# Retention's sample states: read in the mixer, updated in the two FFNs behind it; 72-row spreads and four-strip reads

## The reference, cut to what matters

```
Retention: S_t = gamma_h S_{t-1} + k_t v_t^T, o_t = q_t S_t
q,k (B,L,H,Dk), v (B,L,H,Dv), s0 (B,H,Dk,Dv)        H = 4, Dk = 256, Dv = 512
mLSTM:     C_t = f' C_{t-1} + i' v k^T                H = 4, Dk = 128, Dv = 256
layer 0:   x += 0.5*SwiGLU_1; x += mixer_ab; x += CrossAttn; x += 0.5*SwiGLU_2
layer 1:   x += 0.5*SwiGLU_1; x += mixer_c;  x += CrossAttn; x += 0.5*SwiGLU_2
```

## Time and profile before

| | |
|---|---|
| median of 3 runs | 1909.96 us (1896.08 to 1912.29) |
| the profiled execution | 1907.95 us; span 1906.1 us |
| PE matmul busy | 1786.1 us (94%) |
| DVE, ACT, POOL busy | 1259.7 (66%), 848.1 (44%), 210.9 (11%) |
| mean granted TensorE clock | 0.978 |
| DMA | 361.01 MB, mean 189 GB/s |
| the chain that ended last | PE 69%, DVE 12%, ACT 11%, issue 4%, DMA 3% |

### The profile page before, as it was taken

One profiled execution on the slowest core, in us unless ns is written; L12 is line 12 of the kernel. 1 busy time (PEld: TensorE's weight loads), 2 busy tenths in 40 slices (PEclk: granted clock), 3 DMA queues, 4 the chain that ended last, 5 costly groups with the idle time before them and its releaser, 6 DMA issues.

```text
span 1906.1 us, 34200 instructions
## 1 busy us (share of the span) xinstructions
PE 1786.1 (94%) x13440; PEld 1629.2 (85%) x13440; DVE 1259.7 (66%) x2241; ACT 848.1 (44%) x1156; POOL 210.9 (11%) x305
## 2 busy tenths in 40 slices
PE   7999988998988899999899999999998889899998
PEld 7999988997765555888699999999976788799998
DVE  5765678785886766558567655765555768667653
ACT  5333455364666644332344334433443642344333
POOL 1001101100110111112020001000311031120001
PEclk9999989999999999999999999999999999999999
DMA  8656735444895698657656656665744467756653
GB/s 226 177 167 177 213 109 158 134 133 124 236 288 171 209 294 286 209 199 274 232 149 181 176 162 195 184 186 154 218 137 134 145 240 247 263 151 185 186 154 115
DMA packets 463585, 361.01 MB, mean 189 GB/s; under 512 B 14633, under 2 KB 435781, under 8 KB 463429
## 3 DMA queue, kind: packets, MB, share of 16 engines
q1 hardware_dynamic: 409904, 254.87, 45.7%
q0 software_dynamic: 20288, 71.94, 11.0%
q10 hardware_dynamic: 33280, 32.65, 5.1%
HBM read 320.95 MB, written 38.66 MB: 189 GB/s over the span
## 4 chain that ended last, share of the span: by engine, by line
PE 69%; DVE 12%; ACT 11%; issue 4%; DMA 3%; ACTq 0%; SPq 0%; POOL 0%; DVEq 0%; POOLq 0%
PE psum L263 19%; PE psum L264 18%; PE psum L265 18%; ACT whi L211 4%; DVE wlo L217 4%; DMA raw<-in_w_xkv 2%; PE psum L1723 2%; ACT hb L1503 1%; PE psum L826 1%; PE psum L480 1%; PE psum L2201 1%; PE psum L591 1%; PE psum L2296 1%; PE psum L1350 1%; DVE sb L1745 1%
## 5 line engine op out<-in xcount | busy, mean ns | idle before, releaser
L217 DVE TENSOR_TENSOR wlo<-raw,whi 128x2048 fp32r<-128x2048 f32 (+2 forms) x261 | 553.4, 2120 | 287.9 <-ACT whi L211 287.1
L263 PE MATMUL psum<-xnh,whi 128*128 128x264 f32 x2328 | 676.0, 290 | 6.7 <-DVE ht L1169 4.3
L264 PE MATMUL psum<-xnl,whi 128*128 128x264 f32 x2328 | 665.5, 286 | 0.0
L265 PE MATMUL psum<-xnh,wlo 128*128 128x264 f32 x2328 | 664.5, 285 | 0.0
L211 ACT ACTIVATE whi<-raw 128x2048 fp32r<-128x2048 f32 (+2 forms) x261 | 460.9, 1767 | 134.3 <-DMA raw<-in_w_xkv 61.0
L263 PEld LDWEIGHTS psum<-xnh,whi 128*128 128x128 f32 x2328 | 444.5, 191 | 25.7 <-issue 24.5
L264 PEld LDWEIGHTS psum<-xnl,whi 128*128 128x128 f32 x2328 | 444.9, 191 | 0.3
L265 PEld LDWEIGHTS psum<-xnh,wlo 128*128 128x128 f32 x2328 | 442.4, 190 | 0.0
L263 PE MATMUL psum<-Hh,whi 128*128 128x264 f32 x704 | 200.9, 285 | 0.0
L265 PE MATMUL psum<-Hh,wlo 128*128 128x264 f32 x704 | 200.0, 284 | 0.0
L264 PE MATMUL psum<-Hl,whi 128*128 128x264 f32 x704 | 199.1, 283 | 0.0
(11 more groups left out here) (559 smaller groups left out, 2930.7 us busy)
## 6 DMA issues: line engine op xcount, KB each, us to landing
raw<-in_w_ffn_in SPq DMA_DIRECT2D x176, 512.0 KB, 4.9
raw<-in_w_in_ab SPq DMA_DIRECT2D x88, 512.0 KB, 4.7
raw<-in_w_ffn_out SPq DMA_DIRECT2D x64, 384.0 KB, 4.0
raw<-in_w_ffn_out SPq DMA_DIRECT2D x64, 320.0 KB, 3.4
sb<-in_state_ret POOLq DMA_DIRECT2D x32, 512.0 KB, 5.8
out<-sb ACTq DMA_DIRECT2D x32, 512.0 KB, 3.4
raw<-in_w_out_ab SPq DMA_DIRECT2D x32, 512.0 KB, 5.1
kc<-in_cache_mem_k POOLq DMA_DIRECT2D x32, 512.0 KB, 6.8
```

Source lines behind the costliest of these rows:

```text
L217: nc.vector.tensor_tensor(wlo[:, c % SLOTS, 0:m], raw[:, c % SLOTS, 0:m], whi[:, c % SLOTS, 0:m].bitcast(F32), ALU.subtract).then_inc(lo_d ...
L263: e.matmul(out, a, hi[:, kk, 0:S.cols], start=first, stop=False)
L264: e.matmul(out, a, lo[:, kk, 0:S.cols], start=False, stop=False)
L265: m = e.matmul(out, b, hi[:, kk, 0:S.cols], start=False, stop=final)
```

## The change

- In the mixer a `RetItem` only loads a state and reads it; the next load waits for the read (`s_used`), not for a store. The spread, the decay, the update and the store are gone from there, and so are the rows of v.
- A read is made of four matmuls of 256 columns: two halves of the key dimension (d) times two halves of the value dimension, each into its own 8 rows at 0, 32, 64 and 96 of bank 5 (`lane`). `RetOut` adds the two d-rows with a matmul against a 0/1 matrix (`group_sum`) in place of the transposes, 16 of them over 104 rows. A head now waits for the copy of the head before it. DVE clears bank 5 once.
- `RetKeep` keeps the samples' k and v. `late_work` places, in FFN 2 of layer 0, the rows of v (`LateRows`, 4 groups) and eight loads (`RetLater`) behind chunk 0, and one `RetUpdate` (spread, load of the state six items ahead, decay, update, store) behind chunks 1, 3, .. 21 and behind chunks 1, 4, 7, 10, 13 of its output projection; the other 16 in the same way in FFN 1 of layer 1.
- Rows and spreads use 72 rows (low part at 64) in place of 40, everywhere.
- mLSTM reads alternate between two groups of rows, which are added by matmuls (`pair_sum`) in place of transposes; `RowsOut` is one copy of 104 rows in place of two of 8. Its first loads wait for the late stores.
- `TURNS` becomes (0, 3, 2, 1).

```diff
-            TURNS = (0, 2, 1, 3)
+            TURNS = (0, 3, 2, 1)
...
+        group_sum = cols[0:104, 16:32].rearrange("p (q b) -> p q b", q=2)
+        sel = place("sel", [72, NS], F32R)
...
-        def spread40(e, out, b, rows):
-
-
-            return e.matmul(out, sel[0:40, b:b + 1].to_broadcast([40, P]), rows, start=True, stop=True)
+                    d = S.dst[64:72, j * 512:(j + 1) * 512]
+                    e.tensor_tensor(d, psum[64:72, S.bank0 + j % 2, :], d.bitcast(F32), ALU.subtract).then_inc(rows_lo, 1)
+
+        def spread72(e, out, b, rows):
+
+
+            return e.matmul(out, sel[0:72, b:b + 1].to_broadcast([72, P]), rows, start=True, stop=True)
...
-            row_of = lambda h: slice(64 + 32 * (h % 2), 64 + 32 * (h % 2) + NS)
+            lane = lambda d, half: slice(32 * (2 * d + half), 32 * (2 * d + half) + NS)
+            part_of = lambda h: slice((h % 2) * 256, (h % 2) * 256 + 256)
...
+                    e.memset(psum[:, 5, :], 0.0).then_inc(qk_made, 1)
...
                 def pool(S, e):
                     j = S.i + SB
                     if j < N_RET:
-                        e.wait_ge(s_out[buf(j)], 16 * (j // SB))
+                        e.wait_ge(s_used, S.i + 1)
                         load_s(e, j)
 
                 def pe(S, e):
                     i = S.i
                     b, h = item(i)
-                    v_row(e, i)
                     if i == 0:
                         e.wait_ge(qk_made, 2)
                     if b == 0:
                         e.wait_ge(q_set, h + 1)
-                        if h >= 2:
-                            e.wait_ge(rr_copied, h - 1)
+                        if h >= 1:
+                            e.wait_ge(rr_copied, h)
                     e.wait_ge(s_in[buf(i)], 16 * (i // SB + 1))
                     for d in range(2):
-                        m = e.matmul(psum[row_of(h), 5, :], qm[:, h % 2, d, b * NS:(b + 1) * NS], sb[:, buf(i), d, :],
-                                     start=b == 0 and d == 0, stop=b == NS - 1 and d == 1)
+                        for half in range(2):
+                            m = e.matmul(psum[lane(d, half), 5, part_of(h)], qm[:, h % 2, d, b * NS:(b + 1) * NS], sb[:, buf(i), d, half * 256:half * 256 + 256],
+                                         start=b == 0, stop=b == NS - 1)
                     m.then_inc(s_used, 1)
+
+            keep_v = place("keep_v", [P, 64 + 128], at=norm_at + 2 * T * 4)
+            keep_k = place("keep_k", [P, 8, NS], at=norm_at + 2 * T * 4 + 768)
+            later = place("later", [P, LB, 2, 512], at=REG + 57344)
+            late_in, late_out = s_in[0:4] + hb_in, s_out[0:4] + hb_out
+            late_base = ret_moves[0:4] + [64] * 4
+            late_out_base = [0] * 4 + [64] * 4
+            v_late = place("v_late", [72, 2048], F32R, at=REG + 49152)
+
+            class RetKeep(Stage):
+
+
+                def dve(S, e):
+                    e.memset(keep_v[:, 0:64], 0.0)
+                    e.tensor_copy(keep_v[:, 64:192].rearrange("p (t b) -> p t b", b=NS), vf[:, :, NP:T])
+                    link(e, "dve", e.tensor_copy(keep_k[:, :, :], ks[:, :, :]))
+
+            class LateRows(Rows72):
+
+
+                def __init__(S, ready):
+                    S.dst, S.n, S.bank0, S.ready = v_late, 4, 6, ready
+                    S.r0 = tot["rows"]
+                    tot["rows"] += S.n
+
+                def pe(S, e):
+                    S.ready(e)
+                    for j in range(S.n):
+                        if j >= 2:
+                            e.wait_ge(rows_lo, S.r0 + j - 1)
+                        for q in range(4):
+                            t = 4 * j + q
+                            e.transpose(psum[0:72, S.bank0 + j % 2, q * P:(q + 1) * P], keep_v[:, 8 * t:8 * t + 72], ident[:, :])
+                            m = e.transpose(psum[0:NS, S.bank0 + j % 2, q * P:(q + 1) * P], keep_v[:, 64 + 8 * t:72 + 8 * t], ident[:, :])
+                        m.then_inc(rows_turned, 1)
+
+            def load_late(e, i):
+                e.dma_start(later[:, i % LB, :, :], sv(A["state_ret"], i)).then_inc(late_in[i % LB], 16)
+
+            class RetLater(Stage):
+
+
+                def __init__(S, free, rows):
+                    S.free, S.rows = free, rows
+
+                def pool(S, e):
+                    S.free(e)
+                    for i in range(LB):
+                        load_late(e, i)
+
+                def pe(S, e):
+                    e.wait_ge(rows_lo, S.rows.r0 + S.rows.n)
+
+            class RetUpdate(Stage):
+
+
+                def __init__(S, i):
+                    S.i = i
+
+                def pool(S, e):
+                    i = S.i - 2
+                    if 0 <= i < N_RET - LB:
+                        e.wait_ge(late_out[i % LB], late_out_base[i % LB] + 16 * (i // LB + 1))
+                        load_late(e, i + LB)
+
+                def pe(S, e):
+                    i = S.i
+                    b, h = item(i)
+                    if i >= 2:
+                        e.wait_ge(s_new, i - 1)
+                    spread72(e, psum[:, 6 + i % 2, :], b, v_late[:, h * 512:(h + 1) * 512]).then_inc(vb_done, 1)
 
                 def keep(S, e, i):
                     e.wait_ge(s_new, i + 1)
-                    e.dma_start(sv(O[9], i), sb[:, buf(i), :, :]).then_inc(s_out[buf(i)], 16)
+                    e.dma_start(sv(O[9], i), later[:, i % LB, :, :]).then_inc(late_out[i % LB], 16)
 
                 def act(S, e):
                     i = S.i
-                    if i >= 2:
-                        S.keep(e, i - 2)
-                    e.wait_ge(s_used, i + 1)
-                    v = sb[:, buf(i), :, :]
+                    if i >= 1:
+                        S.keep(e, i - 1)
+                    e.wait_ge(late_in[i % LB], late_base[i % LB] + 16 * (i // LB + 1))
+                    v = later[:, i % LB, :, :]
                     nc.scalar.activation(v, v, ACT.Copy, scale=gam[item(i)[1]]).then_inc(sdec, 1)
-
-                def update(S, e, i):
+                    if i == N_RET - 1:
+                        S.keep(e, i)
+
+                def dve(S, e):
+                    i = S.i
                     b, h = item(i)
                     e.wait_ge(sdec, i + 1)
                     e.wait_ge(vb_done, i + 1)
                     for d in range(2):
-                        v = sb[:, buf(i), d, :]
-                        ins = e.scalar_tensor_tensor(out=v, in0=psum[:, 6 + i % 2, :], scalar=ks[:, 2 * h + d, b:b + 1], in1=v,
+                        v = later[:, i % LB, d, :]
+                        ins = e.scalar_tensor_tensor(out=v, in0=psum[:, 6 + i % 2, :], scalar=keep_k[:, 2 * h + d, b:b + 1], in1=v,
                                                      op0=ALU.mult, op1=ALU.add)
                     ins.then_inc(s_new, 1)
 
-                def dve(S, e):
-                    if S.i >= 1:
-                        S.update(e, S.i - 1)
-
-
-            class RetLast(Stage):
-
-
-                def dve(S, e):
-                    RetItem(N_RET - 1).update(e, N_RET - 1)
+            def late_work(free):
+
+                rows = LateRows(free)
+                items = [RetUpdate(i) for i in range(N_RET)]
+                first = [rows, RetLater(free, rows)]
+                half = N_RET // 2
+                spots = list(range(1, 22, 2)), list(range(1, 16, 3))
+                at = [{}, {}, {}, {}]
+                for n, it in enumerate(items):
+                    f, m = n // half, n % half
+                    j, c = (0, spots[0][m]) if m < len(spots[0]) else (1, spots[1][m - len(spots[0])])
+                    at[2 * f + j].setdefault(c, []).append(it)
+                at[0].setdefault(0, []).extend(first)
+                return at
+            deferred.append(late_work)
...
-                    e.tensor_scalar(rrow[row_of(h), h // 2, :], psum[row_of(h), 5, :], gam[h], None, ALU.mult).then_inc(rr_copied, 1)
+                    e.tensor_scalar(rrow[0:104, h, 0:256], psum[0:104, 5, part_of(h)], gam[h], None, ALU.mult).then_inc(rr_copied, 1)
...
-                    e.wait_ge(s_new, N_RET - 1)
                     for t in range(16):
-                        r = row_of(t // 4)
-                        m = e.transpose(psum[:, 4 + 2 * (t // 4 % 2), t * NS:(t + 1) * NS], rrow[r, t // 8, (t % 4) * P:(t % 4 + 1) * P], ident[r, r])
+                        m = e.matmul(psum[:, 4 + 2 * (t // 4 % 2), t * NS:(t + 1) * NS], rrow[0:104, t // 4, (t % 2) * P:(t % 2 + 1) * P], group_sum[:, t // 2 % 2, :],
+                                     start=True, stop=True)
...
-            ret_at[0] = [v_rows[1], SSDSample(15)]
+            ret_at[0] = [SSDSample(15)]
             ret_at[1] = [SSDEnd(15), SSDOut()]
-            ret_at[2] = [RetStart()]
+            ret_at[2] = [RetKeep(), RetStart()]
...
```

(19 more changed lines are left out.)

84 lines of the change are left out of this document (39 added, 45 removed).

## The result

The kernel after takes 1873.36 us (median of 4 runs, 1872.77 to 1873.97), the kernel before 1907.51 beside it (1896.08 to 1912.29): a ratio of 0.9841, 95% interval 0.9813 to 0.9869. It is faster, by 34 us of 1907 or 1.6%, clear of the scatter; the forecast was 17.5 us less than before, 1890, in a range of 1866 to 1918 that holds the result. A later set gave 0.9843 (0.982 to 0.9865). The profiled execution has a span of 1871.5 us (before: 1906.1).

What follows compares the result with a forecast made beforehand. The prediction took PE, 69% of the chain that ended last, as the bound, with ACT and DVE setting most gate-projection chunks. Mixer 47, FFNs -34, mLSTM 2.5 and TURNS 2 made 17.5 us saved: 1907.95 to 1890 us, range 1866 to 1918.

Steps and rivals of the forecast that it cites:

- part 2: The FFNs, which take over the spreads and updates: 34 us slower, from spreads 20.5, LateRows 11.5 and DMA 2.
- part 1: The mixer, with shorter state reads and without spreads and updates: 47 us saved.
- Output projection: In the mixer: 19 items save 1.7 us each, plus 4.8 us idle, 37 us before new waits and RetOut.
- Gate projection: In the mixer: ACT's chain sets five chunks, so only 15 us of PE's 22 come through; ends 12 to 24.
- LateRows: Behind chunk 0 of FFN 2: PE stands 10 us for low parts, 1.5 more for a slower clock; 11.5 us lost.
- DMA: In the FFNs: 16.8 MB more loads bring the DMA share to 0.87; 2 us lost, ends 0 and 15.
- TURNS: Head order in the v projection: 8.3 us around against 8.6; 2 us saved over 8 chunks, ends -2 and +5.
- A: The forecast itself, chance 0.5: all terms as summed, 1880 to 1902 us.
- B: Whole kernel, chance 0.2: PE's time comes through everywhere, the gate projection giving its 22 us; 1870 us.
- D: Mixer reads, chance 0.03: four strips don't overlap for accumulating reads, 1.3 us x 32 less saved; 1925 us.
- C: FFNs' output projections, chance 0.17: doubled state traffic makes weights late, 30 to 35 us; slower, 1923 us.
- the wash (E): Whole kernel, chance 0.1: stalls at LateRows and at the heads at their bad ends cancel the gain; 1905 us.

Runs made afterwards that it cites:

- e1: The kernel after with all row spreads over 40 rows as before, nothing else changed; 1886.58 us, ratio 0.9901 to the kernel before.
- e9: The kernel after run again unchanged, as the measure for two other runs; 1870.63 us, ratio 0.9843 to the kernel before.
- e6: The kernel after with a finished head's copy directly behind its last read, not half a chunk later; 1869.46 us, ratio 0.9819 to before.
- e11: The kernel after with 40-row spreads, one-strip reads in both mixers and the old head order, so mainly the move; 1909.68 us, ratio 1.0035 to before.
- e3: The kernel after with retention's reads, RetOut's transposes and the wait for head copies as before; 1888.51 us, ratio 0.991 to before.
- e5: The kernel after with the LateRows groups in three places, behind chunks 0, 2 and 4 of FFN 2; 1868.15 us, ratio 0.982 to before.
- e7: The kernel after with late stores, and late loads behind the first eight, cut to 1 of 128 partitions; 1870.44 us, ratio 0.9829 to before.
- e2: The kernel before with 72-row spreads everywhere and nothing else of the change; 1896.98 us, ratio 0.9962 to the kernel before.
- e4: The kernel after with the head order of before, (0, 2, 1, 3); 1874.25 us, ratio 0.9835 to the kernel before.
- e10: The kernel after with the mLSTM's reads in one group of 8 rows per head and transposes, as before; 1878.17 us, ratio 0.9876 to before.

## Why the prediction was right, and where it was not

The side and the mechanism were right: PE's items leave a stretch that PE sets, and come back smaller in one that PE sets too. The sum was half of what came. Of the 17 us that it lacked, 10 are in the FFNs, from one step, and 7 in cross-attention, for which it had no term; the output projection gave 3 more than forecast and the gate projection 4 less, which about cancels by luck. That the range holds the result owes to its width of 52 us.

**The step that failed** is the first of part 2, "32 spreads of 72 rows cost what those of 40 do (the columns are the same 512): 0.43 + 0.10 + 0.11 = 0.64 us each". The three numbers were right for 40 rows, and e1 shows them again in the FFNs. But of the 0.43 only 0.24 are the columns; the rest, the gap ahead and the delay behind are the price of 40 rows between weights of 128, and 72 rows do not pay it. That is 0.4 us x 32 = 13 us; 11.9 measured, or 8.9 against e9. With 40 rows (e1) the two FFNs took 35.6 us, for the 34 of the forecast; with 72 they took 23.7 in after and 26.7 in e9. The rule was cited in part 1 for the reads, where it changed nothing, and not asked of the very edit that the diff makes for every spread. From it came a second miss, "0" for cross-attention: its 8 pairs of spreads cost 0.39 us less each, 3.1 us in layer 0. After gained 7.4 there. Set beside e1 the stretch seems to refute this, for with 40 rows it is shorter still; but its length goes with the granted clock. The windows are of before, after, e1 and e6:

```profile
784.93:966.69 181.76, 167.84 (x1274) 150.57 (x1273) 109.63 (x245) 62.58 (x83) 29.10 (x49) 0.95 0.62 214
735.48:909.87 174.39, 161.49 (x1274) 147.72 (x1273) 109.42 (x245) 62.62 (x83) 29.07 (x49) 0.98 0.65 223
738.57:909.25 170.68, 160.80 (x1274) 144.21 (x1273) 109.22 (x245) 62.59 (x83) 29.05 (x49) 1.00 0.66 228
730.86:908.96 178.10, 165.48 (x1274) 151.26 (x1273) 109.42 (x246) 62.60 (x83) 29.06 (x49) 0.95 0.63 219
```

At the same 0.95 it takes 181.8 us (before) and 180.6 (e11) with 40 rows and 178.1 (e6) with 72, which agrees with the 3.1. The other 4 of after's 7.4 us go with its clock, 0.98 for 0.95. What raised it is open: PE's wait for one load (`mtok`) alone lasts 1.3 to 4.1 us in these traces, and whether waits lower the clock or a lower clock makes the waits was not told apart.

**Output projection** (forecast 29.5 with the waits and RetOut, measured 32.6). The read came out at 0.55 us as forecast, RetOut takes 3.6 for the 3.9 assumed. The waits: 2.2 us at head 2, as forecast, none at head 3. e3 and e11 split it: the spreads and the waits for updates (the idle 4.8) give 15, the strips 18.

**Gate projection** (forecast 15, measured 11.4). Right in kind: ACT and DVE set the chunks, and e3 and e6 show that 16 us of PE's reads more or less change the stretch by 0.7 us. Wrong in the step "in a chunk that ACT and DVE set anyway, so nothing" for head 1's wait: it lasted 4.07 us, the 4 us forecast, and the chunk behind it gave nothing in place of 2.1; in e6, without the wait, that chunk gives 2.5. (The chunk ahead of it gave 0.3 in after and in e6, so its missing 1.8 have another cause, which is open.) Without the wait the gate projection gives 13.6 us. I read it so: PE's statistics feed ACT's root, so a late PE delays the next turn of the chain, and the clock was lower as well; the two were not told apart.

**LateRows** (11.5, measured 11.6 on PE). Every part came as forecast: the stand behind the second group for ACT's and DVE's evictions (4.91 us), the slower transposes behind it, and the wait for the last low part. The eviction times show 10.9 us by the third chunk behind it (13.9 in e9). e5 takes 4.7 to 5.5 of it back.

**DMA** 2 us: e7 gives 0.7 and 1.9, or 3.4 and 2.2 against e9. **POOL**: its late refills delayed nothing that PE had to wait for. **TURNS** (2 us) and **the rows of v** (3): the evictions show 0.6 up to 456.7 and 4.9 from there to 573.6, of which 1.6 come at 476.8, where e2 too has 1.7, from the spreads of B and C. The whole times of e4 cannot tell TURNS from nothing; by the evictions the 0.6 are its worth. **mLSTM** 2.5: 1.5 by the evictions (5.2 in e9), 4 to 6 by e10; not settled.

**The rivals.** A, the forecast's own case, put the time at 1880 to 1902 and the time is 7 us below: what made the difference was none of the mechanisms named. B gave 1870, near to what came, but its mechanism, PE's time coming through in the gate projection, is what e3 refutes. D is out with the first read of 0.55; its price, 1925, is also less than its own 1.3 x 32 = 42 us make, while e3, which has such reads, is 13 us slower than after. C is out with e7, and the wash (E) is what the move alone would have been: e11, 1.0035.

## What to carry to other kernels

- A small matmul between full ones can cost more than its columns: here the spread cost 0.63 us of PE over 40 rows and 0.24 over 72, and the longer operand cost nothing else that the runs show. So try to pad such an operand, and price each form from a row with the same neighbours.
- What such a saving is worth depends on what PE waits for next: in the FFNs it came through, in front of the updates of e2's output projection it did not.
- To move work off one PE-bound stretch onto another gained nothing by itself here (1.0035); it pays where the piece becomes smaller on the way. After a move look for the stands it makes: the first group that waits for its own result, and the copy that stands half a chunk behind its last read. Each was worth about 5 us here.
- A wait on an engine that idles anyway need not be free: here one of 4.07 us cost 2.5.

## What the runs showed of the hardware that was not expected

- The 40-row spread has 0.43 us of its own where the 72-row one has 0.24, with the same 512 columns. Where a read into 8 columns follows, 72 rows make the item 0.2 us shorter (2.14 for 2.34, e2).
- Shorter work on PE can go with a lower clock: with reads of 1.81 us the gate projection ran at a granted clock of 1.00 (e3), with reads of 0.55 at 0.92 (after, e6), and the 11 us less of PE's work shortened it by 0.7 us at most.
- The same cross-attention took from 170.7 us at a granted clock of 1.00 (e1) to 181.8 at 0.95 (before), with the other eleven traces in between and nearly in the order of their clocks. A difference of a few us between two traces is worth checking against the clock first.
- 32 loads and 32 stores of 512 KB, put into four stages that had a DMA share of about 0.6 before, brought it to 0.96 in one stretch. ACT waited 11 times for the input weights of the two FFNs, 13.9 us in all, for once and 2.3 us in before; taking most of the traffic away (e7) gave about 2 us by the ratios.
